# A third gate tile projected inside the S5 stage of a two-layer network, in the bank of the lags

## What is computed

```python
u_l, g_l = jnp.split(h_lat @ w_in, 2, axis=-1)        # w_in: 1024 x 4096
y = y_l                                               # state space model over u, two directions
def glu_out(y, g):
    y = jax.nn.gelu(y)
    ya, yb = jnp.split(y @ w_glu + b_glu, 2, axis=-1)
    return ((ya * jax.nn.sigmoid(yb)) * jax.nn.silu(g)) @ w_out
```

## Time and profile before

| what | value |
|---|---|
| median of 3 runs | 2282.01 us (2280.55 to 2282.4) |
| profiled execution, its time | 2281.87 us |
| profiled execution, its span | 2279.9 us |
| PE busy | 94% of the span |
| DVE, ACT, POOL busy | 58%, 35%, 27% of the span |
| mean granted clock of PE | 0.976 |

### The profile page before, as it was taken

The page is one execution under the profiler, slowest core; times in us unless marked ns, Lnnn a source line. Parts: engine busy times, 40 slices in busy tenths (PEclk is TensorE's granted clock), DMA queues, the critical chain, the costliest instruction groups (busy, mean ns, idle before and its releaser), DMA issues.

```text
span 2279.9 us, 39953 instructions
## 1 busy us (share of the span) xinstructions
PE 2152.7 (94%) x15754; PEld 1563.8 (69%) x15754; DVE 1319.6 (58%) x2345; ACT 788.1 (35%) x1449; POOL 613.6 (27%) x1118
## 2 busy tenths in 40 slices
PE   6998998999998999999999969999998999999997
PEld 6876877756564555555455558888876788888785
DVE  2266664359995444444389868888893333333334
ACT  1335443231103444444300074555443423323223
POOL 0553211410116888888502111111100000000000
PEclk8999999999999999999999989999998999999999
DMA  8321433422452111111154316887864233333221
GB/s 312 102 91 58 150 131 134 158 82 99 157 202 77 55 55 65 56 54 54 49 212 177 144 58 213 249 270 247 274 213 143 84 93 102 93 101 93 92 93 37
DMA packets 105529, 292.48 MB, mean 128 GB/s; under 512 B 12576, under 2 KB 49824, under 8 KB 97152
## 3 DMA queue, kind: packets, MB, share of 16 engines
q1 hardware_dynamic: 93184, 226.10, 30.6%
q0 software_dynamic: 12160, 63.84, 7.4%
HBM read 223.97 MB, written 65.93 MB: 127 GB/s over the span
## 4 chain that ended last, share of the span: by engine, by line
PE 88%; DVE 6%; issue 2%; ACT 2%; DMA 1%; POOL 0%; SPq 0%; DVEq 0%; ACTq 0%; POOLq 0%
PE psum L458 30%; PE psum L1764 8%; PE psum L2452 7%; PE psum L2620 5%; PE psum L2195 5%; PE psum L2231 4%; PE psum L2817 3%; PE psum L2206 3%; PE psum L1039 3%; PE psum L2220 2%; PE psum L2276 2%; PE psum L2267 2%; PE psum L2763 2%; PE psum L293 1%; PE psum L2822 1%
## 5 line engine op out<-in xcount | busy, mean ns | idle before, releaser
L458 PE MATMUL psum<-split,w_split 128*128 128x512 f32 x1632 | 373.1, 390 | 3.7 <-DVE w_split L440 3.7
L458 PEld LDWEIGHTS psum<-split,w_split 128*128 128x128 f32 x1632 | 307.3, 188 | 68.2 <-DVE w_split L440 4.1
L440 DVE TENSOR_TENSOR w_split<-ring,w_split 128x512 fp32r<-128x512 f32 x188 | 133.1, 708 | 323.7 <-ACT w_split L435 323.4
L1983 POOL TENSOR_TENSOR early<-early 128x8 f32<-128x8 f32 (+6 forms) x672 | 276.5, 411 | 52.8
L435 ACT ACTIVATE w_split<-ring 128x512 fp32r<-128x512 f32 x188 | 118.8, 632 | 352.0 <-PE psum L458 348.7
L1764 PE MATMUL psum<-early,ring 128*128 128x512 f32 (+1 forms) x544 | 176.5, 486 | 0.0
L2452 PE MATMUL psum<-gate,ring 128*128 128x512 f32 (+1 forms) x512 | 165.4, 486 | 1.2 <-issue 1.2
L2620 PE MATMUL psum<-h,u_w 128*128 128x256 f32 (+1 forms) x768 | 148.5, 348 | 13.0 <-ACT u_t L2540 11.4
L458 PE MATMUL psum<-h,w_split 128*128 128x512 f32 x624 | 151.0, 403 | 8.5 <-DVE w_split L440 8.5
L1764 PEld LDWEIGHTS psum<-early,ring 128*128 128x128 f32 x544 | 103.7, 191 | 71.8 <-issue 64.7
L458 PEld LDWEIGHTS psum<-h,w_split 128*128 128x128 f32 x624 | 120.4, 193 | 37.7 <-ACT w_split L435 5.4
(11 more groups left out here) (423 smaller groups left out, 3675.9 us busy)
## 6 DMA issues: line engine op xcount, KB each, us to landing
ring<-in_s_glu SPq DMA_DIRECT2D x64, 512.0 KB, 3.5
ring<-in_w_mod SPq DMA_DIRECT2D x48, 512.0 KB, 5.3
made_c_pow<-area POOLq DMA_DIRECT2D x16, 1152.0 KB, 4.9
c_pow<-made_c_pow SPq DMA_DIRECT2D x16, 1152.0 KB, 6.2
ring<-in_s_in SPq DMA_DIRECT2D x32, 512.0 KB, 6.3
made_b_pow<-area POOLq DMA_DIRECT2D x15, 1024.0 KB, 4.8
b_pow<-made_b_pow SPq DMA_DIRECT2D x15, 1024.0 KB, 8.8
ring<-in_w_in SPq DMA_DIRECT2D x29, 512.0 KB, 3.6
```

Source lines behind the costliest of these rows:

```text
L440: nc.vector.tensor_tensor(rounded(buffer(u, 1)), source(u), buffer(u, 0), ALU.subtract).then_inc(dve_done, 1)
L458: ins = nc.tensor.matmul(out, rounded(buffer(u, w)[:, ks]), values(x, k), start=(first and k == 0 and n == 0), stop=(last and k == UNIT_K ...
L1983: nc.gpsimd.tensor_tensor(o, a, b, op).then_inc(pool_done, 1)
```

## The change

The number of gates that are projected inside S5 goes from two to three. Gate 2 takes the place m + 3 = 18, in tile 15, and is put into bank 4 once DVE has copied the last lags out of it. All gates go by a new list of banks, (0, 1, 4, 3), with the period four as before, and the GLU's first product waits for the Silu of gate 14, since that gate lies in bank 4 now. Because the counts in `split_weights`, `u_round_act`, `s5_pool`, `gates_pe`, `gates_act` and `gates_dve` are written in `GATES_AHEAD`, they follow: the two units of gate 2 are split by ACT and POOL in tile 14, `y_store_pool` of tile 13 is issued after the second of them, the gates phase has 13 gates (3 to 15), and there unit 2i + 1 is the second half of gate i + 3.

```diff
-        GATES_AHEAD = 2
+        GATES_AHEAD = 3
+        GATE_BANKS = (0, 1, 4, 3)
...
+        def gate_bank(g):
+            return bank(GATE_BANKS[g % 4])
+
         def gate_ahead_pe(pe, g, k):
...
             if k == 0:
                 pe.wait_ge(*at("s5", "u", KE - 1))
+                if g == 2:
+                    pe.wait_ge(*at("s5", "lag_copy", KE - 1))
             for n, (w, x) in enumerate(((0, 0), (0, 1), (1, 0))):
-                ins = nc.tensor.matmul(bank(g), rounded(u_w[:, u % 4, w, kk * P:(kk + 1) * P]), rounded(h3[:, x, k, :, C_CTX:C_ALL]),
+                ins = nc.tensor.matmul(gate_bank(g), rounded(u_w[:, u % 4, w, kk * P:(kk + 1) * P]), rounded(h3[:, x, k, :, C_CTX:C_ALL]),
...
-                    gate_w_pe(pe, 2 * (i - GATES_AHEAD) + unit, bank(i % 4), h3_latent(unit), unit == 0, unit == 1)
+                    gate_w_pe(pe, 2 * (i - GATES_AHEAD) + unit, gate_bank(i), h3_latent(unit), unit == 0, unit == 1)
...
-            nc.scalar.activation(gates[:, i, :], bank(i % 4), ACT.Silu).then_inc(act_done, 1)
+            nc.scalar.activation(gates[:, i, :], gate_bank(i), ACT.Silu).then_inc(act_done, 1)
...
                 if i == 0:
                     pe.wait_ge(*at("y_split", "rest", KE - 1))
+                    pe.wait_ge(*at("gates", KE - 2))
```

## The result

The changed kernel takes 2304.1 us (median of 5 runs, 2302.53 to 2308.84) against 2282.01 before (5 runs). The ratio is 1.0096 with a 95% interval from 1.0078 to 1.0114: 22 us slower. The profiled execution took 2302.53 us.

A forecast was written before the change was run, and what follows sets the result against it. PE's order of work was taken as the bound, with the 14 gates unbroken on PE. Terms -5.7 + 2.2 + 0.4 + 2.9 + 15.9 + 2.1 = +17.8 on 2281.87 gave 2299.7 us; range 2294 to 2306.

The forecast's parts named there:

- its four terms: Gates phase: one gate less -5.7, gate 4's first wait +2.9, ten later waits +15.9, ACT's longer turns before the GLU +2.1.
- POOL's subtractions: Tile 14: two more subtractions each delay a DVE product between SBUF tiles by 1.08; +2.2 us, bounds 0 and 2.2.
- tile 15: 24 added matmuls make PE slower than DVE for two pairs: +2.2, less 1.8 from the full clock, net +0.4 us.
- What bounds the kernel: Whole chain and gates phase: PE holds 88% of what ended last; one unbroken PE piece of 78.82 us for 14 gates.
- The gate removed: Gates phase: one gate less for PE, -5.7 us.
- the way into the GLU: End of gates phase: GLU starts 11.4 us after ACT's last rounding, not 9.28, from one more ACT turn; +2.1 us.
- The tail at the full clock: End of tile 15: with its products PE has no long gaps, so the last y's matmuls run faster; -1.8 us.
- The wait for the Silu: Gates 5 to 14: PE waits while ACT first rounds a non-urgent unit; 1.59 us each, ten waits, 15.9 us.
- Gate 4 and the clock: Gates 4 and 5, behind the first two waits, might start at the low clock, 2.0 us each; high end only.
- The clock rival: Gates phase: clock falls in every gap, 12 gates cost 2.0 us more each; +24, 2324 us; chance 0.09.
- The rotation rival: Gates phase: the banks' rotation hides the Silu, no gate waits; about -3, 2279 us; chance 0.05.
- The table: Gate 4's first wait: Silu's table load adds 1.28, wait 2.9 by the row; the skill's draining would make it 4.3.

The follow-up runs named there:

- the first experiment: Changed kernel with the Silu of gate i - 1 moved between the roundings of units 2i and 2i + 1 on ACT: 2278.28 us, ratio 0.999.
- the third experiment: Changed kernel with five banks for the gates (0, 1, 4, 3, 2), PE waiting for the Silu of gate i - 5: 2281.23 us, ratio 1.0001.
- new list: Changed kernel with GATES_AHEAD back at 2, keeping banks (0, 1, 4, 3) and the GLU's wait for gate 14: 2280.98 us, ratio 0.999.
- three banks: Kernel before (two gates ahead) with three banks for the gates in place of four: 2301.84 us, ratio 1.0079.
- two splits more: Kernel before with the last gate's weights split a second time in tile 14 by ACT and POOL, unused by PE: 2278.73 us, one run.
- the early table: Changed kernel with a one-column Silu on ACT behind the first two roundings, to load the table there: 2294.04 us, one run.
- the three-ahead version with the new order: Changed kernel with Silu between roundings, y's splits two a turn, GLU's first units split early, even shares in tile 15: 2269.43 us, ratio 0.9954.

## Why the prediction was right, step by step

The sign, the cause and the size hold: 2299.7 was forecast for a profiled execution of 2302.53 and a median of 2304.1. Of the change's own part, 17.8 were forecast and 19.4 measured. Some of that closeness is luck: errors cancel. The gates phase came out 2.8 above its four terms (18.0 for -5.7 + 2.9 + 15.9 + 2.1 = 15.2), POOL's subtractions 1.2 below theirs, and tile 15 met its net +0.4 (2.12 - 1.33 - 0.4) with a low clock inside it that the prediction had not seen.

- *What bounds the kernel* was read rightly from the chain: with PE in one piece, whatever broke that piece had to be paid in full.
- *The gate removed*, -5.7. Not seen alone; without waits the phase is 3.4 to 3.7 shorter (the first and the third experiment), for the reason that the prediction gave for the way into the GLU: ACT has one turn of 2.14 more behind its last rounding.
- *POOL's subtractions*, +2.2 forecast, +0.96 measured. Mis-sized: the price of one was right, but only one of the two meets a DVE product between SBUF tiles. The rows gave no warning of it: in tile 12 and in tile 13 of before the second subtraction does delay a DVE product between SBUF tiles (in tile 13 to 1.31 us, at 1666.06, in place of 0.42).
- *Tile 15*, +2.2 and -1.8 forecast. DVE came 1.31 and 0.81 later, 2.12, but the shares alone make 0.7 of it (the first experiment). The prediction counted from the turning at 1703.94, and before that PE had run at the low clock:

```profile
1699.00:1701.00 2.00, 1.58 (x16) 0.61 0.56 135
1701.00:1703.00 2.00, 2.00 (x21) 0.53 0.72 188
```

In that trace the turning starts 2.8 us after the scan of tile 15's first state; in the first experiment, with the clock at 1.00, it starts 1.3 after it (1712.93 and 1711.65). The 1.5 between them is most of the 2.2. That the forecast of 2.2 held is luck: the clock of the changed kernel was low at nearly the same place (its turning starts 2.7 after the scan).
- *The tail at the full clock* gave 1.33 up to the turning and 0.4 in the turning and after, 1.7 for the 1.8 forecast. That the products in tile 15 bring it is not shown: all six profiles with a third gate ran the last y's first 16 matmuls in 1.09, but so did three of the five with two gates ahead (new list, three banks, two splits more), which have no product there; the other two took 1.97. With two ahead and the full clock S5's end is 39.11. POOL's 0.96 makes it 40.07, as in the kernel with the two splits more, and the uneven shares 40.76, as in the first experiment.
- *The wait for the Silu*: 1.43 us in eleven gates, as written, and 2.71 in the first. By the starts, a wait costs 7.38 - 5.69 = 1.69 a gate and not 1.59. A gate's 24 matmuls between two waits take 0.1 more than in an unbroken piece; why is open. Ten gates: 16.9 for 15.9.
- *Gate 4 and the clock*: 8.91 us from its start to the next, 1.53 above the period. The prediction kept this out of the sum and in the upper end. That is the largest term that was missing, and the early table has shown it.
- *The way into the GLU*: 11.4 us behind the last rounding, as forecast to the tenth.
- *The clock rival* came true for one gate of twelve. *The rotation rival* fell, but its rule did not. (Its 2.7 for the tiles 14 and 15 is 2.6 by the prediction's own terms, which changes nothing.) The Trainium skill (Perfetto Trace Analysis, Matmuls in Optimizing Tensor Performance) says that rotating banks lets one bank's evacuation overlap the next group's products. The prediction held against it that the Silu stands behind its rounding "whatever the number of banks". So it does, but with five banks PE waits for the Silu of gate i - 5 and not for that one. Five banks gave the overlap here with 81.7 us, and four did not with 103.4: the rotation must reach past the consumer's place in its own list.
- *The table*: ACT's Silu starts 0.01 us behind its load of 1.28, and PE's wait was 2.71, which leaves no room for the 1.4 us more that the Trainium skill (ScalarE: Activation LUTs, What ACT_TABLE_LOAD costs) adds for draining. Here the trace does not agree.

**What lies outside the change.** Of the 2.7 us that the profile of after has less behind the gates, 2.6 come from one place, PE's restart after its wait of 3.2 us between the GLU and the last projection, shown below. The 4.2 us more ahead of tile 14 stay open: 1.3 of them lie ahead of S5, and the code there is the same. The medians differ by 22.1, which is the 19.4 and 2.7 more; of that no part was tested.

## What to carry to other kernels

An engine that works through a list written by hand serves a deadline by its place in the list, not by its speed. When a count that shifts one list against another is changed (tiles ahead, buffers, banks), write out for one turn which item the producer waits for and what stands ahead of it in the consumer's list; here one item too many was worth some 20 us, and moving it cost nothing. And work moved out of a full phase into an idle stretch pays only what the phase's end lets through: look at what starts the next phase before counting the gain.

## What was not expected of the hardware

The same wait was followed by different clocks. Between the GLU and the last projection PE waits 3.22 or 3.23 us in every profile. In the kernel before, in that with the new list, and in the three-ahead version with the new order, what follows is this:

```profile
2164.84 11.06 PE L458 MATMUL psum<-h,w_split 128*128 128x512 f32 x36 [3.23 <-DVE w_split L440]
```

```profile
2165.66 8.45 PE L458 MATMUL psum<-h,w_split 128*128 128x512 f32 x36 [3.23 <-DVE w_split L440]
```

```profile
2153.03 11.28 PE L458 MATMUL psum<-h,w_split 128*128 128x512 f32 x36 [3.23 <-DVE w_split L440]
```

36 matmuls in 11.06, 8.45 and 11.28 us: at the low clock in part, at the full one, at the low one in part. In the eleven profiles they took 8.42 to 8.45 six times and 9.75 to 11.28 five times, so a wait of that length is followed by 0 or up to 2.8 us of loss with no cause in the code that was found, while none of the 45 waits of 1.43 us changed the clock, and 2.71 did in all three profiles that have it (7.48, 7.49 and 7.37 us for its 24 matmuls; in the third it is gate 3). A wait of 2.32 us at the GLU's start (two ahead, three banks) was followed by the low clock too.

A DVE product between two SBUF tiles that starts beside a running subtraction of POOL ends a little less than its own time after POOL does, as if it had waited for it. The product that began at 1687.48 ended at 1689.13, and POOL's subtraction ran from 1687.14 to 1688.58: 0.55 behind it, for a product that takes 0.69. In the other order POOL is the one that takes longer: the product of 1694.79 had begun 0.17 ahead of POOL's subtraction, kept its 0.69, and the subtraction took 1.66 in place of 1.44.
